# First six projections on x times the norm's weights, the root multiplied in at copying out

## The reference, cut to what matters

```python
def rmsnorm(t, g):
    tf = t.astype(jnp.float32)
    tf = tf * lax.rsqrt(jnp.mean(tf * tf, axis=-1, keepdims=True) + EPS)
    return tf.astype(t.dtype) * g

h = rmsnorm(x, norm_g)
proj = h @ w_in
(q_lat, kv_lat, k_pe, c_b, c_c, c_u, q_mem,
 g_attn, g_conv, g_mem, r) = split_cols(proj, IN_SIZES)
q = (rmsnorm(q_lat, q_norm_g) @ w_uq).reshape(B, S, N_HEADS_MLA, QK_HEAD_DIM)
kv = (rmsnorm(kv_lat, kv_norm_g) @ w_ukv)...
```

## Time and profile before

| | us |
|---|---|
| median of 3 runs | 2270.02 (2269.95 to 2271.81) |
| profiled execution | 2269.04 |
| its span | 2267.2 |
| TensorE busy | 2210.5 |
| VectorE busy | 1304.5 |
| ScalarE busy | 902.4 |
| GpSimd busy | 1244.4 |

### The profile page before, as it was taken

One profiled execution on the slowest core, in us unless ns is written; L12 is line 12 of the kernel. 1 busy time (PEld: TensorE's weight loads), 2 busy tenths in 40 slices (PEclk: granted clock), 3 DMA queues, 4 the chain that ended last, 5 costly groups with the idle time before them and its releaser, 6 DMA issues.

```text
span 2267.2 us, 29807 instructions
## 1 busy us (share of the span) xinstructions
PE 2210.5 (97%) x9694; PEld 1736.1 (77%) x9694; DVE 1304.5 (58%) x2401; ACT 902.4 (40%) x1429; POOL 1244.4 (55%) x824
## 2 busy tenths in 40 slices
PE   8999999999999998999999999999999999999998
PEld 5666665777777776788888888888887888888886
DVE  5454332225643685797676665222223988888887
ACT  4565544335544554434323333222222433333333
POOL 3432022244434332268888888888886655555553
PEclk9999999999999999999999999999999999999999
DMA  7664233325423221245666666666656999999996
GB/s 244 200 212 150 79 89 125 90 92 171 149 75 103 76 85 47 93 94 90 147 144 148 140 147 145 144 148 127 113 105 190 351 325 358 349 356 350 353 356 241
DMA packets 240050, 396.96 MB, mean 175 GB/s; under 512 B 87992, under 2 KB 162744, under 8 KB 239712
## 3 DMA queue, kind: packets, MB, share of 16 engines
q1 hardware_dynamic: 161088, 328.48, 44.6%
q0 software_dynamic: 78880, 67.50, 14.9%
HBM read 330.60 MB, written 61.01 MB: 173 GB/s over the span
## 4 chain that ended last, share of the span: by engine, by line
PE 58%; DVE 2%; ACT 0%; DMA 0%; issue 0%; SPq 0%; DVEq 0%; ACTq 0%
PE bank L1474 30%; PE bank L1485 23%; PE bank L1230 4%; PE bank L1457 0%; ACT staged L1525 0%; DMA tail<-gates 0%; DVE u_split L2278 0%; DVE low L1966 0%; DVE tail L2210 0%; DVE tail L2245 0%; DVE tail L2243 0%; DVE tail L2246 0%; DVE tail L2189 0%; DVE staged L2192 0%; DVE tail L2199 0%
## 5 line engine op out<-in xcount | busy, mean ns | idle before, releaser
L1107 POOL DMA_INDIRECT gates<-low x384 | 627.9, 1635 | 140.3 <-issue 116.8
L1474 PE MATMUL bank<-h_high,u_tiles_split 128*128 128x512 f32 x2048 | 630.9, 389 | 2.2 <-DVE u_tiles_split L2177 2.2
L1075 POOL TENSOR_TENSOR u_split<-blocks,u_split 128x1024 fp32r<-128x1024 f32 (+1 forms) x102 | 245.2, 2404 | 586.7 <-ACT u_split L1629 558.0
L1230 PE MATMUL bank<-h_high,u_split 128*128 128x512 f32 x1664 | 540.5, 400 | 10.8 <-POOL u_split L1075 6.8
L1485 PE MATMUL bank<-v_split,a_split 128*128 128x512 f32 x2286 | 520.2, 390 | 2.8 <-DVE a_split L2317 2.8
L1485 PEld LDWEIGHTS bank<-v_split,a_split 128*128 128x128 f32 x2286 | 430.1, 188 | 92.9 <-DVE v_split L2314 3.1
L1474 PEld LDWEIGHTS bank<-h_high,u_tiles_split 128*128 128x128 f32 x2048 | 384.6, 188 | 81.9 <-issue 2.4
L1474 PE MATMUL bank<-h_low,u_tiles_split 128*128 128x512 f32 x1024 | 398.6, 389 | 0.0
L1230 PEld LDWEIGHTS bank<-h_high,u_split 128*128 128x128 f32 x1664 | 313.7, 189 | 86.6 <-issue 21.3
L2177 DVE TENSOR_TENSOR u_tiles_split<-tail,u_tiles_split 128x1024 fp32r<-128x1024 f32 x128 | 157.1, 1228 | 361.5 <-ACT u_tiles_split L1816 360.6
L1230 PE MATMUL bank<-h_low,u_split 128*128 128x512 f32 (+1 forms) x704 | 274.4, 390 | 0.0
(11 more groups left out here) (232 smaller groups left out, 2360.9 us busy)
## 6 DMA issues: line engine op xcount, KB each, us to landing
tail<-in_uT SPq DMA_DIRECT2D x128, 512.0 KB, 3.8
tail<-in_v SPq DMA_DIRECT2D x128, 512.0 KB, 5.4
gates<-blocks SPq DMA_DIRECT2D x32, 768.0 KB, 5.8
tail<-gates SPq DMA_DIRECT2D x128, 192.0 KB, 5.6
kept_hidden<-tail SPq DMA_DIRECT2D x96, 192.0 KB, 1.9
tail<-kept_hidden SPq DMA_DIRECT2D x96, 192.0 KB, 5.7
blocks<-in_r SPq DMA_DIRECT2D x24, 512.0 KB, 4.0
blocks<-in_conv SPq DMA_DIRECT2D x16, 512.0 KB, 4.4
```

Source lines behind the costliest of these rows:

```text
L1075: nc.gpsimd.tensor_tensor(flat(u, 1)[:, 0:n], ring[:, loads[0] % NW, 0:n], flat(u, 0)[:, 0:n].bitcast(F32), ALU.subtract).then_inc(s_wlo, 1)
L1107: nc.gpsimd.indirect_dma_start(gate_elements, bass.IndirectOffsetOnAxis(ap=expert_no[tb][:, k:k + 1], axis=0), expert_gate[tb][:, k:k + 1] ...
L1230: last = mm(ps[0:m, :], flat(u, part)[:, k * m:(k + 1) * m], x, start=(k == 0 and j == 0), stop=(k == nk - 1 and j == 2))
L1474: last = mm(bank[slot % 2][:, :], U4[:, slot, w, k, :], x[:, k, :], start=(k == 0 and x is hh and w == 0), stop=(k == KD - 1 and w == 1))
```

## The change

- The first six projections (lat 0 to 4, kpe) take x times the norm's weights, without the root. VectorE makes high parts by a scaling (`early_high`) and low parts by a scaling and subtraction (`early_low`), into buffers that are free at that time. Their copies-out go from ScalarE to VectorE, as a product with the root (`scaled`).
- TensorE does lat 0 and lat 1 by passes: all high by high products, then low weights, then, behind the norm's sums, the low inputs.
- The normalised h, with its high and low parts, is still made, for the conv tiles and what follows, behind the copies-out of lat 0 and 1 and around that of lat 2. The angles come behind the copy-out of lat 3.
- ScalarE's weight casts for the first three tiles stand between the squares; GpSimd's subtractions follow them.
- SyncE loads weight tiles 0 and 1 before the second and fourth piece of x, and the constants last. The filling matmuls go, two f32 matmuls on x come at the start.
- The root of this norm has rows of its own, and the tile of zeros is elsewhere; the copy-out of mk 0 waits for the stores from it.

```diff
-    for k in range(1, KD - 1):
-        STEPS.append(("sum", "x", k))
+    for kind, ks in (("early_high", (0, 1)), ("early_low", (0,)), ("early_high", (2, 3)), ("sum", (1,)),
+                     ("early_low", (1, 2)), ("early_high", (4, 5)), ("sum", (2, 3)), ("early_low", (3,)),
+                     ("early_high", (6, 7)), ("sum", (4, 5, 6)), ("early_low", (4, 5, 6, 7))):
+        for k in ks:
+            STEPS.append((kind, "x", k))
+    for k in range(KD):
+        STEPS.append(("square", "x", k))
+        if k in (3, 5, 7):
+            STEPS.append(("high_weights", (k - 3) // 2))
+    part(0, 0, KD)
+    part(1, 0, KD)
+    part(0, KD, 2 * KD)
+    part(1, KD, 2 * KD)
     STEPS.append(("norm", "x"))
+    for i in range(2):
+        tile("lat", i, KD, P)
+    scaled(0)
+    scaled(1)
+    STEPS.append(("normalise", "x", 0, 4))
+    tile("lat", 2, KD, P)
+    scaled(2)
+    STEPS.append(("normalise", "x", 4, KD))
     STEPS.append(("high_h", "x"))
+    tile("lat", 3, KD, P)
+    scaled(3)
     STEPS.append(("angles",))
-    side_by_side("lat")
-    for i in range(2, QL + KVL):
-        tile("lat", i, KD, P)
+    tile("lat", 4, KD, P)
+    scaled(4)
     tile("kpe", 0, KD, QKD)
+    scaled(5)
...
             for c in range(4):
+                if c % 2:
+                    sp.dma_start(ring[:, c // 2, 0:LOADS[c // 2][2]], t_in["lat"][c // 2]).then_inc(s_w[c // 2], 16)
                 sp.dma_start(xT[:, 2 * c:2 * c + 2, :], t_in["xT"][:, 2 * c:2 * c + 2, :]).then_inc(s_x[c], 16)
                 if c == 0:
-                    sp.dma_start(const, t_in["const"][:, 0:NKEEP]).then_inc(s_const, 16)
                     sp.dma_start(cols, t_in["cols"]).then_inc(s_par, 16)
+            sp.dma_start(const, t_in["const"][:, 0:NKEEP]).then_inc(s_const, 16)
...
                 if n >= 2 and k_begin == 0:
-                    pe.wait_ge(s_evac, ev(n - 2))
+                    wait_evacuated(pe, n - 2)
...
+                    if by_pass:
+                        for c in range(k_begin, k_end):
+                            j, k = c // KD, c % KD
+                            if i == 0 and j == 0:
+                                pe.wait_ge(s_early_high, early_no("x", k))
+                            if c == KD:
+                                pe.wait_ge(s_wlo, u + 1)
+                            if i == 0 and j == 2:
+                                pe.wait_ge(s_early_low, early_no("x", k))
+                            last = mm(ps[:, :], flat(u, j % 2)[:, k * P:(k + 1) * P],
+                                      early_low("x", k) if j == 2 else early_high("x", k),
+                                      start=(c == 0), stop=(c == 3 * KD - 1))
+                        return last
...
                     if key == "x":
-                        keep_busy(i, 3)
+                        pe.wait_ge(s_const, 16)
...
-            pe.wait_ge(s_const, 16)
+            pe.wait_ge(s_x[0], 16)
+            for _ in range(2):
+                mm(ax[1][:, :], xT[:, 0, 0:P], xT[:, 0, :], start=True, stop=True)
...
+            def early_parts(key, k, low):
+                x, g = xT[:, k, :], col({"x": "norm", "x2": "norm1", "h2": "norm2"}[key], k)
+                if not low:
+                    if key == "x":
+                        dve.wait_ge(s_x[k // 2], 16)
...
+                    V.tensor_scalar(early_high(key, k), x, g, None, ALU.mult).then_inc(s_early_high, 1)
+                    return
+                dve.wait_ge(s_early_high, early_no(key, k))
+                V.scalar_tensor_tensor(early_low(key, k), x, g, early_high(key, k).bitcast(F32),
+                                       ALU.mult, ALU.subtract).then_inc(s_early_low, 1)
+
+            def scaled(n):
+                kind, i, _ = PROJ[n]
+                dve.wait_ge(s_rs, norm_no["x"])
+                dve.wait_ge(s_proj, n + 1)
+                ps = pj[n % 2]
+                if kind == "lat":
+                    V.tensor_tensor(lat[:, i, :], ps[:, :], roots("x"), ALU.mult).then_inc(s_scaled, 1)
+                    return
+                link(V.tensor_tensor(lat[0:QKD, 5, :], ps[0:QKD, :], roots("x")[0:QKD, :], ALU.mult))
+                V.tensor_tensor(lat[0:ROPE, 5, :], ps[NOPE:QKD, :], roots("x")[NOPE:QKD, :], ALU.mult)\
+                    .then_inc(s_scaled, 1)
...
-        zeros = region(HH + 6144 + 3 * T, TD)
+        zeros = region(mkT_off, TD)
...
                 elif kind == "mk":
+                    if i == 0:
+                        act.wait_ge(s_zero, 16 * NKEYS // 4)
```

More of the change, by code:

```diff
@@ L537, in program @@
         o = HH + 12288
+        root_rows = region(spare_off, T)
         oT = region(o, 12 * T, 12)
@@ L749, in program @@
         pi = {(k, i): n for n, (k, i, _) in enumerate(PROJ)}
-        evacuated = [not (kind == "v2" and i % 4 < 3) for kind, i, _ in PROJ]
+        evacuated = [not (kind == "v2" and i % 4 < 3 or kind in ("lat", "kpe")) for kind, i, _ in PROJ]
         def ev(n):
@@ L1113, in _ @@
             for s in STEPS:
-                if s[0] == "high_h" and s[1] == "x":
+                if s[0] == "norm" and s[1] == "x":
                     for u in split_after[-1]:
@@ L1193, in proj @@
                 kind, i, loads = PROJ[n]
+                by_pass = kind == "lat" and i < 2
                 k_begin = begun.get(n, 0)
-                k_end = part[1] if part else KD
+                k_end = part[1] if part else 3 * KD if by_pass else KD
                 if part:
@@ L1228, in split @@
                         high = oh[t // 8][:, t % 8, :] if kind == "br" else hh[:, t, :]
-                        for j, (part, x) in enumerate(((0, high), (0, x_low[:, t, :]), (1, high))):
+                        low = x_low[:, t, :]
+                        if early:
+                            high, low = early_high(early, t), early_low(early, t)
+                            if kind == "wq" and i == 0:
+                                pe.wait_ge(s_early_low, early_no("h2", t))
+                        for j, (part, x) in enumerate(((0, high), (0, low), (1, high))):
                             last = mm(ps[0:m, :], flat(u, part)[:, k * m:(k + 1) * m], x,
@@ L1330, in norm @@
                     mm(ax[i % 2][:, :], ones, sq[:, j % NQ, :], start=False, stop=True).then_inc(s_aux, 1)
+                    if key in ():
+                        for tb in range(TB):
+                            to, tokens = ax[(i + 1) % 2][:, 2 * tb:2 * tb + 2], slice(tb * P, (tb + 1) * P)
+                            mm(to, rs[:, tokens], ones[:, 0:2], start=True, stop=False)
+                            last = mm(to, sq[:, j % NQ, tokens], ones[:, 0:2], start=False, stop=True)
+                        last.then_inc(s_tok, 1)
                     if key == "h2":
@@ L1679, in norm @@
                 rows = min(width, P)
-                if ("sq", key) not in STEPS and key not in ("x2", "h2", "mem"):
+                if ("sq", key) not in STEPS and key not in ("x", "x2", "h2", "mem"):
                     squares(key)
[L1682 to L1685, removed]
+                if key == "h2":
                     high_weights(waiting.pop(0))
@@ L1691, in norm @@
                     act.wait_ge(s_norm, j - 1)
-                r = rs[0:rows, 0:N]
+                r = roots(key)[0:rows, 0:N]
                 if key == "x":
@@ L1933, in norm @@
                 dve.wait_ge(s_rs, j)
-                r = rs[0:rows, 0:N]
-                for k in range(nk):
+                r = roots(key)[0:rows, 0:N]
+                for k in ks or range(nk):
                     if key == "x":
@@ L2144, in _ @@
                     settle()
-                if s[0] == "norm":
+                if s[0] == "norm" and s[1] in ("x", ):
+                    pass
+                elif s[0] == "norm":
                     norm(s[1])
+                elif s[0] == "normalise":
+                    norm(s[1], range(s[2], s[3]))
+                elif s[0] in ("early_high", "early_low"):
+                    early_parts(s[1], s[2], s[0] == "early_low")
+                elif s[0] == "scaled":
+                    scaled(s[1])
+                elif s[0] == "scaled_values":
+                    scaled_values()
                 elif s[0] == "split":
```

76 lines of the change are left out of this document (64 added, 12 removed).

## The result

The changed kernel takes 2282.89 us (median of 5 runs, 2282.31 to 2283.4), the kernel before 2271.81 (5 runs), a ratio of 1.0049 with an interval of 1.0037 to 1.006. It is slower by 11 us; the forecast was 2280.7, 10.7 slower. The profiled execution took 2283.22 us, span 2281.4, against 2269.04 and 2267.2.

A forecast was written before the change was run, and what follows sets the result against it. The prediction took TensorE, 97% busy, as the bound. Conv 1's 10.7 us delay added to the profiled 2269.04 gave 2279.7, and 0.98 for the runs' median made 2280.7 us; range 2274 to 2284.5.

The forecast's parts named there:

- The bound: Whole kernel: TensorE is busy 97% of the span, so the change matters only through TensorE's stretches of waiting.
- The start: Tiles 0 and 1: first matmul at 12.2 instead of 20.59, but they end at 32.7, 1.0 us later than before.
- VectorE's line: VectorE's queue from 32.7: norm tiles, copies, angles and stops delay conv 0 to 64.2; TensorE waits 8.3 us.
- The clock: TensorE's lower clock after idling: 1.0 us more at the start, 1.7 us at conv 0.
- The second conv tile: Conv 1 on TensorE starts at 72.8 instead of 62.13, 10.7 us later, carried to the end.
- The choice on the high parts: VectorE's high-part scalings at the start: 0.43 us each, stopping behind GpSimd; the sum is then 10.7 us.
- the rival that they run past: High parts 4 to 7 take 0.60 us but pass GpSimd, last ready at 18.0: +8, 2278 us; chance 0.2.
- Rival 1: First 75 us: no stops between VectorE and GpSimd, conv 1 at 56.4, 5.7 us earlier, 2264.3 us; chance 0.07.
- Rival 2: First 75 us: half of the seven or so blocks fall in gaps, 0 to +4 us, about 2272.5; chance 0.12.
- Rival 4: After the start: later waits, such as TensorE's 6.8 us for u_split, absorb part: +6, 2276 us; chance 0.09.

The follow-up runs named there:

- e0: The changed kernel itself, unaltered, run again beside other follow-up kernels on one chip: 2282.48 us, ratio 1.0051 to the kernel before.
- e1: The changed kernel with GpSimd's first eight weight subtractions cut to 16 columns instead of 1024, for measuring only: 2269.90 us, ratio 0.9987 to the kernel before.
- e6: The changed kernel with VectorE instead of GpSimd subtracting the first three weight tiles: 2276.86 us, ratio 1.0024 to the kernel before.
- e4: The changed kernel with eight unread f32 matmuls on TensorE behind the counts, in the wait before conv 0: 2279.77 us, ratio 1.0036 to the kernel before.
- e7: The changed kernel with the edits of both e5 and e6: 2267.35 us, ratio 0.9978 to the kernel before.
- e3: The changed kernel with the 17 angle instructions behind lat 4's copy-out instead of ahead of it: 2279.48 us, ratio 1.0037 to the kernel before.
- e5: The changed kernel with angles halved, behind lat 4's and kpe's copies-out, and key-value squares ahead of the rotary tables: 2272.93 us, ratio 1.0004 to the kernel before.
- e2: The kernel before the change, with GpSimd's first eight weight subtractions cut to 16 columns: 2270.50 us, ratio 0.9993 to the uncut kernel before.

## Why the prediction was right

- **The bound.** TensorE at 97% was the right thing to start from; only its waits moved.
- **The start.** Forecast 12.2 for the first matmul, 20.2 for the last high part, 32.7 for the end of tiles 0 and 1. Measured 13.08, 20.4 and 33.33. The 0.9 us at the first is the second piece of x (8.9 forecast, 9.88 here, 8.49 in e0). The alternation of VectorE and GpSimd was right in its sum and is shown by e1 and e6: without the two subtractions there the holes are gone. It was not right in each row: I had the second weight cast at 16.2, it ran at 14.71, since one sum slipped through first.
- **VectorE's line.** Copy of lat 3 forecast to end at 48.3 ahead of kpe's subtraction; measured to end at 48.81. The line began 0.9 us late (copy of tile 1 at 33.60, forecast 32.7), and the stops beside the subtractions for lat 3 and lat 4 took 3.0 us (4.43 less 1.41) where 3.5 were forecast. Angles from 49.7 to 63.5, measured 48.84 to 63.40: the start is 0.9 early because kpe's subtraction fell beside the angles' first instruction (1.57 us), and not ahead of it. Conv 0 forecast 64.2, measured 64.18; the wait 8.3 and 7.68. So close a hit has luck in it: these errors cancel, and e0 had 62.88.
- **The clock.** One stretch for 1.7 us at conv 0: e4 shows 2.0 by the tile. The other stretch, at the start, was sized at 1.0 and cost somewhat more: from the last high part to the third tile TensorE took 12.9 us (20.4 to 33.33), where the sum had 11.5 and 1.0. The first trace has no record of the clock before 24.0 us, and a 1.00 printed for that time says nothing; that of e0 has it, at half level in the first pass and full behind it:

```profile
19.00:22.00 3.00, 3.00 (x8) 2.35 (x8) 2.79 (x6) 1.56 (x2) 0.65 (x1) 0.50 0.67 257
23.00:26.00 3.00, 3.00 (x15) 2.45 (x14) 2.99 (x3) 0.00 (x0) 1.12 (x1) 1.00 0.00 0
```

The hole is not needed for it: in e7 the first pass has none, and the clock is 0.50 from 13 to 18 us.
- **The second conv tile.** 72.8 forecast, 73.05 measured; 10.7 and 10.9 later.
- **The choice on the high parts.** Two of them took 0.88 us (0.43 apart), as taken, and not the 0.60 apiece of the rival. That they stop behind GpSimd isn't shown by a long row of their own, since in this trace the ones near a subtraction came behind stopped sums and low parts. The rival that they run past had as its test a last high part before 18.5; it came at 20.4. Copies-out have one input in PSUM and one in SBUF and don't stop: that of tile 1 ran at 33.60 within a subtraction's time (32.89 on) in 0.69 us. The row that the prediction read for this (89.10 in the earlier trace rows) shows less, since it had begun before the subtraction. The Trainium skill, "SBUF — State Buffer", section "Who interferes with whom", says that a VectorE instruction with at most one SBUF input, outside the modes that use two ports, does not contend with GpSimd; the copy at 33.60 agrees.
- **Rival 1** priced a start without any stop at conv 1 at 56.4; e1, where there is none, has 57.70. The mechanism's size was right, and it didn't happen.
- **Rival 2**, half of the stops in gaps, did not happen: with and without the subtractions the second conv tile lies 15.4 us apart (73.05, and 57.70 in e1), near the 16.4 that the forecast had for all of them.
- **Rival 4**, something taken up later, did not happen: TensorE's waits for GpSimd's u_split in the later stretches are the same 6.8 us as in the earlier trace rows, moved with it. The profiled executions lie 14.2 us apart at the end, though, 3.3 more than at the second conv tile. Some 1.7 of it is a low clock behind a wait that the kernel before has as well (below, the stretch behind this wait, after first and then before); 0.9 came where the last stage begins and 0.4 near 862 us; these are not explained. The medians, 11.1 us apart, show that it is mostly the luck of the two executions: that of before lies 2.8 us under the median of its five runs.

```profile
723.00:729.00 6.00, 5.94 (x19) 4.75 (x20) 0.00 (x0) 0.00 (x0) 2.37 (x1) 0.72 0.30 98
```

```profile
712.00:718.00 6.00, 5.96 (x28) 5.01 (x29) 0.00 (x0) 0.20 (x1) 2.40 (x1) 1.00 0.29 98
```

- **Left open.** What the two f32 matmuls at the start, the removed filling matmuls and the moved tile of zeros cost by themselves was not tried; a part of a microsecond could stand in them.

The same clock probably explains why e1 gained 14.1 us at the second conv tile and 12.6 in the median. Its lead over the kernel before was still 4.2 us at a table load of ScalarE at 638.91 (643.10 before), 0.5 at one at 1037.04 (1037.55), and at one at 1065.31 (1064.20) it was 1.1 behind: 5.3 us lost. Between them the waits of TensorE are the same in kind and size, but the clock isn't (first e1, then the kernel before):

```profile
640.00:800.00 160.00, 153.02 (x736) 116.09 (x736) 79.10 (x162) 76.09 (x161) 57.49 (x43) 0.98 0.29 85
800.00:1060.00 260.00, 245.04 (x1197) 193.93 (x1202) 197.28 (x562) 109.27 (x189) 115.58 (x66) 0.97 0.30 76
```

```profile
640.00:800.00 160.00, 151.74 (x738) 114.38 (x737) 78.62 (x160) 78.57 (x163) 59.12 (x43) 1.00 0.30 88
800.00:1060.00 260.00, 245.03 (x1214) 194.16 (x1213) 198.23 (x566) 110.06 (x190) 115.07 (x66) 0.98 0.30 77
```

One or two hundredths of 160 and 260 us are 3 and 3 us, by rounded figures, against 5.3 lost. That is read from one execution each; the runs' spread fits it (e1 from 2264.05 to 2272.15).

## What to carry to other kernels

An earlier start on the busiest engine is worth nothing by itself: follow the work that now has to be done by the second engine, in its queue order, up to the next place where the first one waits for it, and add what stands in the way there. When work moves onto an engine that is stopped by a neighbour, price each of its instructions beside the neighbour's, and ask whether it would be cheaper to do the neighbour's work on it too (1.22 us against a stop of 2.1). Before an instruction that frees a buffer goes behind a long row of others, look at who else waits for that row: moving it once (e3) uncovered the next wait, moving both (e5) paid.

## What the runs showed of the hardware

- The same wait of TensorE, 3.30 us after the change and 3.32 before, brought a granted clock of 0.72 over the six microseconds behind it in one trace and 1.00 in the other. The traces of e0, e1, e2, e5, e6 and e7 have a low stretch there too, those of e3 and e4 don't. Whether this wait cost its length alone or more could not be told from its length.
- The second piece of x was in use at times from 8.28 (e6) to 9.88 us (the first trace of the change) with the same loads ahead of it in the queue. A 512 KB load's landing can't be forecast to better than about a microsecond from one trace.
- One VectorE instruction with two inputs in SBUF, a 128x1024 subtraction with a rounded output, takes 1.22 us; GpSimd takes 2.4 for it, and a 128x512 sum or low part of VectorE beside it took some 2.1 us longer.
